# Time mixing on one core: the order of the state carries and the products of the next pair of heads on TensorE

## The reference, cut to what matters

```python
def step(S, inp):
    r_t, d_t, k_t, v_t, kk_t, a_t = inp
    Sk = jnp.einsum('bhij,bhj->bhi', S, kk_t)
    S = S * d_t[:, :, None, :] - Sk[..., None] * (kk_t * a_t)[:, :, None, :] + v_t[..., None] * k_t[:, :, None, :]
    return S, jnp.einsum('bhij,bhj->bhi', S, r_t)
```

## Time and profile before

| | |
|---|---|
| time, median of 3 runs | 1491.59 us (1490.55 to 1494.34) |
| the profiled execution | 1493.52 us |
| its span | 1491.9 us |
| mean granted TensorE clock | 0.994 of full speed |
| busy over the span | TensorE 98%, its weight loads 72%, VectorE 57%, ScalarE 37%, GpSimd 25% |

### The profile page before, as it was taken

How to read it: one execution, slowest core, us unless ns; L and a number is a source line. 1 busy time by engine, 2 the same in 40 slices (tenths; PEclk the granted TensorE clock), 3 DMA queues, 4 the chain that set the end, 5 groups by cost and what they waited for, 6 DMA issues and landing times.

```text
span 1491.9 us, 36424 instructions
## 1 busy us (share of the span) xinstructions
PE 1457.3 (98%) x14550; PEld 1079.6 (72%) x14550; DVE 857.5 (57%) x1713; ACT 555.6 (37%) x1355; POOL 371.2 (25%) x483
## 2 busy tenths in 40 slices
PE   6999999999999999999999999999999999999998
PEld 4555577667888888777777777777777777777753
DVE  3153556558777777656677676767676522023533
ACT  3056545452222222244554646354545232210000
POOL 0000041230111111116131313222131046356452
PEclk9999999999999999999999999999999999999999
DMA  9913699833465566511112212121112226343311
GB/s 318 325 51 101 168 254 281 240 100 111 122 153 155 151 156 154 139 31 45 40 41 47 54 44 55 33 52 41 45 39 45 67 64 190 84 144 84 120 43 50
DMA packets 191541, 165.42 MB, mean 111 GB/s; under 512 B 38554, under 2 KB 169626, under 8 KB 190348
## 3 DMA queue, kind: packets, MB, share of 16 engines
q1 hardware_dynamic: 182364, 128.21, 31.0%
q0 software_dynamic: 8352, 32.52, 7.2%
q10 hardware_dynamic: 656, 2.36, 0.5%
HBM read 136.97 MB, written 26.08 MB: 109 GB/s over the span
## 4 chain that ended last, share of the span: by engine, by line
PE 86%; DVE 7%; ACT 2%; DVEq 2%; issue 1%; DMA 1%; POOL 0%; POOLq 0%; SPq 0%; ACTq 0%
PE me_bank L3252 13%; PE rw_bank L1894 11%; PE sa_psOs L1229 8%; PE sa_psS L1182 8%; PE pr_psZ L742 3%; PE me_bank L3290 3%; PE fr_bankL L309 3%; PE fr_bankL L248 3%; PE rw_bank L1930 2%; DVE rw_gram L2754 2%; PE pr_psS L730 2%; PE sa_psT L1192 2%; PE rw_bank L1906 2%; PE sa_psS L1171 1%; PE pr_psO L763 1%
## 5 line engine op out<-in xcount | busy, mean ns | idle before, releaser
L1894 PE MATMUL rw_bank<-hT,big 128*128 128x288 f32 x336 | 94.1, 419 | 0.0
L1290 ACT COPY kpe<-sa_psS 128x512 f32<-128x512 f32 x64 | 34.4, 589 | 138.1 <-PE sa_psS L1182 138.1
L1019 POOL DMA_DIRECT2D big<-in_cache_kv x68 | 37.6, 552 | 151.7 <-issue 151.7
L742 PE MATMUL pr_psZ<-hT,qlT 128*128 128x288 f32 x256 | 74.6, 412 | 0.6 <-DVE pr_zraw L847 0.6
L1894 PEld LDWEIGHTS rw_bank<-hT,big 128*128 128x128 f32 x336 | 59.7, 189 | 16.0 <-ACT big L2405 1.7
L3328 ACT COPY big<-me_bank 128x288 f32<-128x288 f32 x42 | 16.7, 398 | 144.8 <-PE me_bank L3252 141.7
L1019 POOL DMA_DIRECT2D pages<-in_cache_kv x68 | 37.5, 552 | 119.4 <-issue 119.4
L742 PEld LDWEIGHTS pr_psZ<-hT,qlT 128*128 128x128 f32 x256 | 47.3, 191 | 21.4 <-issue 9.5
L1386 DVE TENSOR_TENSOR sa_ST<-sa_psT,kinvp 128x512 f32<-128x512 f32 x64 | 42.9, 679 | 30.6 <-PE sa_psT L1192 30.5
L1229 PE MATMUL sa_psOs<-big,sa_ST 128*128 128x257 f32 x256 | 60.3, 386 | 0.0
L1229 PE MATMUL sa_psOs<-pages,sa_ST 128*128 128x257 f32 x256 | 60.3, 385 | 0.0
(11 more groups left out here) (653 smaller groups left out, 3719.1 us busy)
## 6 DMA issues: line engine op xcount, KB each, us to landing
big<-in_w_in SPq DMA_DIRECT2D x44, 512.0 KB, 4.0
big<-in_cache_kv POOLq DMA_DIRECT2D x68, 128.0 KB, 3.9
pages<-in_cache_kv POOLq DMA_DIRECT2D x68, 128.0 KB, 3.1
fr_wada<-in_w_ada SPq DMA_DIRECT2D x8, 1024.0 KB, 11.4
big<-in_cache_kv SPq DMA_DIRECT2D x60, 128.0 KB, 2.9
pages<-in_cache_kv SPq DMA_DIRECT2D x60, 128.0 KB, 3.0
qk_scratch<-oaT SPq DMA_DIRECT2D x32, 192.0 KB, 2.6
fr_wada<-in_w_ada SPq DMA_DIRECT2D x2, 2048.0 KB, 11.7
```

The source lines that it names most:

```text
L742: last = nc.tensor.matmul(psZ[h][:, 0:HT], M.wz[hp % 2][:, k, :], M.hT[:, k, h * HT:(h + 1) * HT], start=(k == 0), stop=(k == KT - 1))
L1019: e.dma_start(M.pages[s % 2][q * QP:(q + 1) * QP, g, :, 0:KL], src).then_inc(landed, 16)
L1894: last = mm(into, held, moving, start=(k == 0 and n in (1, 2, 7)), stop=(k == K4 - 1), skip_group_check=True)
```

## The change

On TensorE alone, in the order of the end of each pair: the second and the third carry follow the first one directly, each with the source and own sums of the next chunk behind it. M6, the bonus sums and M5 come behind the third carry. The product M3, which stood in two halves around `last_state` and `out_to_tokens`, stands in one piece behind them. In the last pair the eight gate steps stand behind the third carry in one piece, and the eight steps of the z projection behind `out_to_tokens`. No instruction is added, removed or changed in shape.

```diff
                 own_out(0)
                 own_out(1)
                 carry(i, 1)
+                carry(i, 2)
+                carry(i, 3).then_inc(o_mm, 1)
                 if more:
                     multiply(p, VZ, 6)
-                else:
-                    gate_parts(range(56, 60))
-                carry(i, 2)
-                if more:
                     bonus_sums(p)
                     multiply(p, VZ, 5)
                 else:
-                    gate_parts(range(60, 64))
-                carry(i, 3).then_inc(o_mm, 1)
-                if more:
-                    multiply(p, VZ, 3, range(0, 2))
-                else:
-                    project_z(i, range(0, 4))
+                    gate_parts(range(56, 64))
                 last_state(i)
                 out_to_tokens(i)
                 if more:
-                    multiply(p, VZ, 3, range(2, 4))
-                else:
-                    project_z(i, range(4, 8))
+                    multiply(p, VZ, 3)
+                else:
+                    project_z(i, range(0, 8))
```

## The result

| | before | changed |
|---|---|---|
| time, median of 4 runs each | 1491.14 us | 1501.02 us |
| range | 1490.55 to 1494.34 | 1500.25 to 1502.92 |
| ratio, 95% interval | | 1.0064 (1.0050 to 1.0077) |
| profiled execution, its span | 1493.52, 1491.9 | 1501.40, 1499.7 |
| TensorE busy, mean granted clock | 98%, 0.994 | 97%, 0.995 |

The changed kernel is slower by 9.9 us at the medians, 7.5 to 11.5 us by the interval. The forecast was 10.9 us. The two profiled executions are only 7.9 us apart, because they differ ahead of the change as well: TensorE reaches the first carry of pair 0, up to which both kernels do the same, at 730.47 us in the one before and at 728.71 in the changed one.

What follows compares the result with a forecast made beforehand. TensorE was taken to bound the kernel: its own instruction list plus any added waits. The terms, 7 x 1.37 + 1.62 - 0.3 = 10.9 us, gave a forecast of 1502.5 us, range 1498.7 to 1506.5.

Steps and rivals of the forecast that it cites:

- Step 1: Second carry directly behind the first: TensorE waits for VectorE's S2, a new wait of 0.52 us.
- Step 2: Third carry directly behind the second: no wait, since chunk 3's sources and sums cover S3; uncovered it would cost 0.8.
- Step 3: S4 queued behind the factors on VectorE: costs nothing, as last_state, which needs it, leaves 2 us of cover.
- Step 4: M6, bonus sums and M5 in one run behind the third carry: 1.94 + 0.10, 0.97 and 1.94 us.
- Step 5: out_to_tokens behind M5 and last_state: waits for L2506, queued behind L2405 on ScalarE, a new wait of 1.20 us.
- One sign of being wrong: In the changed profile, L2136, forecast about 1.2 us idle, waits well under 1 us.
- Step 6: Transposes, then M3 in one piece: 0.54 and 2.04 us; next grams start 1.37 us later per pair.
- Given back: VectorE's centring and masked copies behind the transposes: 0.04 us per pair recovered, 0.3 in all; bounds 0 and 1.0 per pair.
- VectorE's chain: Rival: VectorE's chain absorbs the delay, no change; a pair would lose 0.4 us, 3 in all, 1494.7; chance 0.05.
- Tile changes: Rival: boundaries between full-size and small tiles cost 0.4 us each; a pair would lose 0.2, 1493.3; chance 0.03.
- The third, faster: Rival: both waits vanish and the 0.45 us saved per pair remains, 3.6 us in all, 1488.0; chance 0.02.
- entering: On TensorE, going to full-size tiles from 64-row ones: costs 0.10 us.

Runs made afterwards that it cites:

- S2 experiment: Against the changed kernel, VectorE makes S2 ahead of the masked product instead of behind it; ratio to the kernel before 1.0032 (1.0014 to 1.0050).
- both orders: Against the changed kernel, ScalarE copies the output bank early and VectorE makes S2 ahead of the masked product; ratio to before 0.9991, again 0.9995.
- M3 split: Against the changed kernel, M3 (last pair: z product) is cut in two, first half between M5 and last_state; ratio to before 1.0044 (1.0030 to 1.0059).
- last-pair kernel: Against the kernel with both orders, VectorE makes the last pair's S3 too ahead of the masked product; ratio to before 0.9991, again 0.9985.

## Why the prediction was right, point by point

- **What bounds the kernel.** TensorE's list plus its waits. Shown: from the grams of one pair to the first carry of the next the changed kernel takes 57.52 us (69.77 less 12.25) where the one before takes 57.51 (68.61 less 11.10), in the shortest distance from one first carry to the next of each. Such a distance was forecast to grow by 1.3 to 1.4 us and grew by 1.16. Nothing of the added waits was given back.
- **Step 1,** the second carry: 0.52 us. The trace has 1.83 from carry to carry, the computed 1.31 + 0.52; shown by the S2 experiment, which takes 0.53 away. In pair 5 it costs 0.35 more, which I had not put in: VectorE is late there by as much before the change too, under M6.
- **Step 2,** no wait of the third carry: right (1.31 from the second to the third).
- **Step 3,** S4 behind the factors: right, and without price by experiment.
- **Step 4,** the run of products: M6 starts 0.48 us behind the third carry, the bonus sums 2.04 behind M6, M5 0.98 behind these and `last_state` 1.94 behind M5, as computed to 0.01.
- **Step 5,** the output copy, is the term that was mis-sized: 1.20 us forecast, 1.03 measured. I took the 0.49 us from L2405 to L2506 for what ScalarE's queue needs. In the changed trace the same two copies start 0.29 apart (807.49, 807.78). Before, L2506 had been waiting for the third carry, whose last products end at 807.75, 0.05 ahead of the copy; 0.2 of the 0.49 us were the wait for it. The trace before had the right price too, in two copies of which the second waited for nothing (805.37, 805.66). The last pair has the same error (1.62 forecast, 1.41 measured). One sign of being wrong was that L2136 waits well under 1 us: the profile's bracket says 0.87, and the distance of the starts 1.03. TensorE and ScalarE before:

```profile
805.37 0.40 ACT L2522 COPY rw_bonus<-rw_bank 128x288 f32<-128x288 f32 x1 [2.08 <-PE rw_bank L1950]
805.66 0.41 ACT L2523 COPY rw_bonus<-rw_bank 128x288 f32<-128x288 f32 x1
807.36 0.39 PE L2120 MATMUL rw_bank<-rw_RT,rw_S 64*64 64x128 f32 x4
```

- **Step 6:** the transposes took 0.49 us with the wait ahead of them, not 0.54. M3 took 2.03, where 2.04 was forecast.
- **Given back:** 0.3 us forecast, none seen. The first masked copy starts only 0.69 us later against the pair's first carry (12.74 before, 13.43 now), while the grams start 1.15 later: the rest was slack of VectorE's, which now waits 0.43 us for TensorE. It was not TensorE's to have back: TensorE's own wait behind these copies (L1991) is still 0.2 per pair.
- **The sum:** 7 x 1.15 + 0.35 + 1.41 = 9.8 us by the traces, 9.9 by the medians, 10.9 forecast. The mechanism is the forecast one. That the sum is only 1.1 too high is in part luck: the output copy and the transposes were forecast some 1.8 us too dear over the eight pairs, and 0.3 that did not come back and 0.35 in pair 5 make up for some of it.
- **The rivals.** VectorE's chain absorbs nothing of TensorE's delay. Tile changes cost 0.1, not 0.4. The third, faster, fell for the reason given (two other engines' orders), and its price was nearly right: with both orders changed, 0.26 us per pair is left of the 0.45, the rest being M3's new wait and late weights (0.1 each).

## What to carry to other kernels

On an engine that is full, products between dependent steps can be the cover for the hand-overs to the other engines, as they were here. Before they are moved away, read where in the other engines' own orders the awaited instruction stands. Here the data was ready for five microseconds, and TensorE waited on an order. A distance between two instructions of one queue is a price of the queue only if the second one waited for nothing else.

## What the runs showed of the hardware that was not expected

- A product whose wait ends last starts with its weight load at the same moment, and takes 0.10 us more than one whose weights went ahead (2.14 against 2.03 us for M3), though no tile size changes there. The same is to be seen at the changes of tile size: the first weights of M6, behind the carries' small tiles, start with the product at 802.33 in the changed trace, while those of M6's next products start 0.24 ahead (803.16 for 803.40):

```profile
802.33 0.78 PEld L1894 LDWEIGHTS rw_bank<-rw_free_c,big 128*128 128x128 f32 x4 [0.17 <-issue]
803.16 0.43 PEld L1894 LDWEIGHTS rw_bank<-rw_free_d,big 128*128 128x128 f32 x2
```

So part or all of what I called entering may be this; the runs don't separate the two.

- TensorE shows single gaps of 0.3 to 1.0 us in its own issue among the small 32-row products (L1991, L2010), 0.3 to 1.9 us in all from execution to execution of otherwise equal kernels; the one of 0.8 in the earlier trace rows is such a one. In one trace (M3 split) a product that takes 2.21 us elsewhere took 3.90. The cause of either isn't known. A larger part of why 2 us are hard to time here lies ahead of the time mix's pairs: TensorE reaches the first carry of pair 0 at 726.4 to 731.7 us in the fourteen traces, with nothing changed up to there.
- The masked product takes 1.96 to 2.08 us in the last pair and 1.23 in the others, in every trace. GpSimd is at work beside it only there. In the trace before:

```profile
1218.51 1.27 POOL L3136 TENSOR_TENSOR me_arena<-me_arena,big 128x512 f32<-128x512 f32 x1
1218.82 2.05 DVE L2832 TENSOR_TENSOR rw_uvm<-uv,pick 128x1024 f32<-128x1024 f32 x1
1219.74 2.25 POOL L3137 TENSOR_TENSOR big<-big 128x512 f32<-128x512 f32 x1
```

The rows look like taking turns: VectorE's ends 1.09 us behind the end of the GpSimd product that began ahead of it, and the next GpSimd product, 2.25 us long instead of 1.27, ends 1.12 behind VectorE's. In the last-pair kernel no GpSimd product follows at once: the one that began first keeps its 1.27 us, and VectorE's still takes 2.08. No run moves the two apart, so this is read from the traces, not tried.
